# Latent keys ahead of nope queries, output units on five banks with two more weight places, gated rows in two steps, low weights by GpSimd in halves

## The reference

```python
# latent attention (8 heads): q from a 384-wide latent, k and v from a 128-wide one
q = (rms_norm(cq, q_norm_g) @ w_uq).reshape(B_, T, MLA_HEADS, dqk)      # nope 128 + rope 64
kv = (rms_norm(ckv, kv_norm_g) @ w_ukv).reshape(B_, T, MLA_HEADS, 256)  # k nope 128, v 128
p = jax.nn.softmax(q @ k * scale); o = p @ v
y = jnp.concatenate([a, b], axis=-1) * jax.nn.silu(gate)
x = x + y @ w_out

# retention (4 heads of 256 keys, 512 values)
o = ((o - mu) * lax.rsqrt(var + NORM_EPS)).reshape(B_, T, RET_V) * gn_g
x = x + (o * jax.nn.silu(gate)) @ w_out

return rms_norm(x, final_norm_g)
```

## Time and profile before

| | |
|---|---|
| median of 3 runs | 1727.99 us (1726.3 to 1729.07) |
| profiled execution | 1727.9 us, its span 1726.0 us |
| busy: PE, DVE, ACT, POOL | 1655.1, 1036.1, 798.5, 710.0 us |
| DMA | 166.87 MB, mean 97 GB/s |
| matmuls | 7340, granted clock 0.988 of full in the mean |

### The profile page before, as it was taken

One profiled execution on the slowest core, in us unless ns is written; L12 is line 12 of the kernel. 1 busy time (PEld: TensorE's weight loads), 2 busy tenths in 40 slices (PEclk: granted clock), 3 DMA queues, 4 the chain that ended last, 5 costly groups with the idle time before them and its releaser, 6 DMA issues.

```text
span 1726.0 us, 19471 instructions
## 1 busy us (share of the span) xinstructions
PE 1655.1 (96%) x7340; PEld 1343.7 (78%) x7340; DVE 1036.1 (60%) x1173; ACT 798.5 (46%) x1001; POOL 710.0 (41%) x325
## 2 busy tenths in 40 slices
PE   3999999999989999999999999999899999999997
PEld 2778787877778888888887888777788787887875
DVE  6777788777637918816633767566337564255642
ACT  2665565666444425423342333666554443244442
POOL 1233343433355444444464443444364252442523
PEclk7999999999989999999999999999999999999999
DMA  9333333332233332332322231211133131331312
GB/s 363 134 111 123 122 116 117 96 124 86 73 104 98 96 99 86 101 131 90 97 83 90 88 104 60 70 54 55 38 98 98 37 110 40 109 96 42 105 49 73
DMA packets 46460, 166.87 MB, mean 97 GB/s; under 512 B 5152, under 2 KB 5280, under 8 KB 45856
## 3 DMA queue, kind: packets, MB, share of 16 engines
q1 hardware_dynamic: 46368, 165.63, 29.4%
HBM read 163.52 MB, written 2.10 MB: 96 GB/s over the span
## 4 chain that ended last, share of the span: by engine, by line
PE 84%; DVE 11%; ACT 2%; issue 1%; DMA 1%; POOL 1%; SPq 0%; DVEq 0%; ACTq 0%
PE lin L625 15%; PE lin L627 15%; PE lin L626 15%; PE big L625 7%; PE big L627 7%; PE big L626 7%; DVE scr L1538 1%; DVE cq_lo L1640 1%; DVE tmp L1667 1%; DVE tmp L2130 1%; PE big L742 1%; DVE tmp L1686 1%; PE big L744 1%; PE big L1033 1%; PE big L1032 1%
## 5 line engine op out<-in xcount | busy, mean ns | idle before, releaser
L599 POOL TENSOR_TENSOR w_lo<-raw,w_hi 128x1024 fp32r<-128x1024 f32 (+1 forms) x215 | 530.7, 2472 | 730.5 <-ACT w_hi L1069 730.3
L625 PE MATMUL lin<-h_hi,w_hi 128*128 128x512 f32 x952 | 375.5, 394 | 6.9 <-POOL w_lo L599 3.9
L627 PE MATMUL lin<-h_hi,w_lo 128*128 128x512 f32 x952 | 371.5, 390 | 0.0
L626 PE MATMUL lin<-h_lo,w_hi 128*128 128x512 f32 x952 | 371.2, 390 | 0.0
L1069 ACT ACTIVATE w_hi<-raw 128x1024 fp32r<-128x1024 f32 (+1 forms) x215 | 223.9, 1041 | 161.0 <-PE m_b L643 49.2
L625 PEld LDWEIGHTS lin<-h_hi,w_hi 128*128 128x128 f32 x952 | 179.1, 188 | 46.4 <-POOL w_lo L599 6.5
L627 PEld LDWEIGHTS lin<-h_hi,w_lo 128*128 128x128 f32 x952 | 179.0, 188 | 38.0
L626 PEld LDWEIGHTS lin<-h_lo,w_hi 128*128 128x128 f32 x952 | 179.2, 188 | 37.0 <-issue 0.7
L599 POOL TENSOR_TENSOR qk_hl<-raw,qk_hl 128x1024 fp32r<-128x1024 f32 (+1 forms) x44 | 109.4, 2490 | 164.7 <-ACT qk_hl L1069 164.7
L625 PE MATMUL lin<-y_hi,w_hi 128*128 128x512 f32 x324 | 127.3, 393 | 5.6 <-DVE y_lo L2135 3.0
L627 PE MATMUL lin<-y_hi,w_lo 128*128 128x512 f32 x324 | 126.1, 389 | 0.0
(11 more groups left out here) (455 smaller groups left out, 3217.1 us busy)
## 6 DMA issues: line engine op xcount, KB each, us to landing
raw<-weights SPq DMA_DIRECT2D x245, 512.0 KB, 3.6
slab<-ada SPq DMA_DIRECT2D x32, 512.0 KB, 4.5
scr<-ada SPq DMA_DIRECT2D x16, 512.0 KB, 6.3
raw<-weights SPq DMA_DIRECT2D x10, 256.0 KB, 2.8
x<-x_t SPq DMA_DIRECT2D x2, 1024.0 KB, 6.1
out_t<-scr SPq DMA_DIRECT2D x8, 256.0 KB, 2.0
raw<-weights SPq DMA_DIRECT2D x4, 448.0 KB, 3.4
rgw<-rg_w SPq DMA_DIRECT2D x1, 1024.0 KB, 7.3
```

Of the source, the lines that this page charges most:

```text
L599: nc.gpsimd.tensor_tensor(lo[:, 0:w], raw[:, s, 0:w], hi[:, 0:w].bitcast(F32), ALU.subtract).then_inc(w_split, 1)
L625: nc.tensor.matmul(psum_of(n), wh, hi(k), start=(k == 0), stop=False)
L626: nc.tensor.matmul(psum_of(n), wh, lo(k), start=False, stop=False)
L627: last = nc.tensor.matmul(psum_of(n), wl, hi(k), start=False, stop=(k == nk - 1))
```

## The change

1. GpSimd makes the low part of an entry wider than 512 in two instructions. The first raises `w_half`, for which nobody waits; the second raises `w_split`.
2. For the first three groups of residual units the squares are added two entries later in GpSimd's stream.
3. In latent attention `kn` comes ahead of `qn`, on every engine. ScalarE copies weights once in each head, behind both high parts, at most three entries past the gate's, and no more at the head's end.
4. `a_out` units take five banks. Two more weight places, in `cq_hi` and `cq_lo`, are open from `a_out` 0 to `rv` 2, free once `qn` 7 is done. Parts of units 2 and 3 stand before and behind the last value products; PE waits for all eight residuals before retention.
5. In retention ScalarE calls `split_ahead` between the second and the third gated row.
6. The four gated rows use four buffers, and VectorE makes the next product before the low part.
7. The last norm: ScalarE premultiplies rows 3, 4 and 5 by the gain, writes the root to `m_b` (PSUM) and then to `rstd`; VectorE multiplies five rows, GpSimd three.

```diff
 def home_plan():
+    windows = ((("w_out", 3), ("p_out", 6), None), (("a_out", 0), ("rv", 2), ("qn", HEADS - 1)))
...
-WIDE = ("w_out", "ff_g", "ff_v", "ff_down", "kr", "cq", "ckv", "u", "pool", "pgate", "p_out")
+WIDE = ("w_out", "ff_g", "ff_v", "ff_down", "kr", "cq", "ckv", "u", "pool", "pgate", "p_out", "a_out")
...
+        if (kind, j) == ("a_out", 0):
+            turn[ring] = 0
...
 # GpSimd
+                if w > 4 * P:
+                    nc.gpsimd.tensor_tensor(lo[:, 0:4 * P], raw[:, s, 0:4 * P], hi[:, 0:4 * P].bitcast(F32),
+                                            ALU.subtract).then_inc(w_half, 1)
+                at = 4 * P if w > 4 * P else 0
+                nc.gpsimd.tensor_tensor(lo[:, at:w], raw[:, s, at:w], hi[:, at:w].bitcast(F32),
                                         ALU.subtract).then_inc(w_split, 1)
                 for r, f in enumerate(OUT_UNITS):
-                    if PACK[UNIT[f]] + 1 + NR <= e < PACK[UNIT[f]] + 6 + NR:
-                        add_square(r, e - NR - PACK[UNIT[f]])
+                    m = e - PACK[UNIT[f]] - (NR + SPARE if r < 3 else NR)
+                    if 1 <= m < (7 if r < 3 else 6):
+                        add_square(r, m)
...
+            pool.wait_ge(out_gained, len(OUT_POOL))
+            pool.wait_ge(norm_rooted, 8)
+            for k in OUT_POOL:
+                nc.gpsimd.tensor_tensor(scr[:, k], scr[:, k], rstd[:], ALU.mult).then_inc(out_pool, 1)
...
 # PE
+                unit("kn", h, lambda k: cq_hi[:, 3], lambda k: cq_lo[:, 3])
                 unit("qn", h, CH, CL)
-                unit("kn", h, lambda k: cq_hi[:, 3], lambda k: cq_lo[:, 3])
...
             shares_turned(g, 3)
+            pe.wait_ge(p_exp, 4 * HEADS)
+            unit("a_out", 2, YH, YL, part=range(3))
             latent_products(g)
+            unit("a_out", 2, YH, YL, part=range(3, 7))
+            unit("a_out", 3, YH, YL, part=range(7))
             for m in range(8):
                 unit("a_out", m, YH, YL, ready=None if m else mixed_values,
-                     part=range(7, DK) if m < 2 else None)
+                     part=range(7, DK) if m < 4 else None)
+            pe.wait_ge(resa_done, 8)
...
 # ScalarE, latent attention
-                split_ahead(UNIT[("agate", h)])
+                split_ahead(UNIT[("agate", h)], 3)
...
-                split_ahead(following)
+            split_ahead(UNIT[("a_out", 0)])
...
 # ScalarE, gated rows
-                    nc.scalar.activation(y_hi[:, 4 * (h % 2) + c], tmp[:, c % 2], ACT.Copy).then_inc(yr_high, 1)
+                    nc.scalar.activation(y_hi[:, 4 * (h % 2) + c], tmp[:, c], ACT.Copy).then_inc(yr_high, 1)
                     act.wait_ge(yr_high, counted(yr_high))
+                    if c == 1:
+                        split_ahead(UNIT[("r_out", 8 * (h // 2)) if h % 2 else ("rq", 2 * h + 2)])
...
+            nc.scalar.activation(m_b[:], rstd[:], ACT.Exp, scale=-0.5).then_inc(norm_rooted, 1)
+            act.wait_ge(norm_rooted, counted(norm_rooted))
+            nc.scalar.activation(rstd[:], rstd[:], ACT.Exp, scale=-0.5).then_inc(norm_rooted, 1)
...
 # VectorE, last norm
-            for k in range(DK):
-                v.scalar_tensor_tensor(out=scr[:, k], in0=x[:, k], scalar=p_("final_norm_g", k), in1=rstd[:],
+            for k in OUT_DVE:
+                v.scalar_tensor_tensor(out=scr[:, k], in0=x[:, k], scalar=p_("final_norm_g", k), in1=m_b[:],
```

More of the change, by code:

```diff
@@ L102, in ring_plan @@
     for h in range(HEADS):
-        units += [("qn", h, 3), ("kn", h, 1)]
+        units += [("kn", h, 1), ("qn", h, 3)]
         if h % 2 and h < HEADS - 1:
@@ L216, in build @@
         w_high = sem("w_high")
+        w_half = sem("w_half")
         w_split = sem("w_split")
@@ L1057, in _, with split_ahead @@
             issued = [0]
-            def split_ahead(n):
-                while issued[0] < NE and (PRIOR[issued[0]] is None or PRIOR[issued[0]] < n):
+            def split_ahead(n, entries=NE):
+                while issued[0] < min(NE, PACK[n] + entries + 1) and (PRIOR[issued[0]] is None or PRIOR[issued[0]] < n):
                     e = issued[0]
```

92 lines of the change are left out of this document (56 added, 36 removed).

## The result

The changed kernel takes 1708.47 us in the median of 4 runs (1707.64 to 1710.79), the kernel before 1728.42 (1726.30 to 1729.07): a ratio of 0.9889, 95% interval 0.9872 to 0.9906. That is 20 us less; the forecast was 16.3 less, 1711.6. The profiled execution of the changed kernel is the slowest of its four (1710.79); its span is 1709.0 us, 17.0 under that of before.

What follows compares the result with a forecast made beforehand. TensorE bounds the kernel, busy 1655.1 of 1726.0 us, so only its 71 us of standing can be won. The terms sum to -15.2, with tails of -1.1 to -16.3: 1727.9 becomes 1711.6 us, range 1704 to 1720.

Steps and rivals of the forecast that it cites:

- Low weights in halves: GpSimd's split low parts: -4.4 us at first-stage suffix waits, +0.3 at the first norm apply, +0.2 for two later tiles.
- The other three are 1.1 each and vanish, and of the longest 1.1 go: First-stage suffix waits of PE: three end, the longest of 1.9 us loses 1.1; together -4.4 us.
- Elsewhere VectorE often has two such instructions in a row, which then meet one half each, and nothing is won: Outside the first stage, the halved low parts were to win VectorE nothing; the first norm apply was put at +0.3 us.
- (c): Rival: slower, as halves hold VectorE twice; 20 us lost against 16.3 won, 1731 us; chance 0.07.
- (d): Rival: halves do nothing for VectorE, as GpSimd keeps its hold over both; 1716 us; chance 0.08.
- Squares two entries later: At w_out's norm: root 0.3 us earlier, norm apply meets no tile, 0.8; -1.1 us. At ff_down and a_out 0.
- Keys ahead of queries: Latent attention: -2.9 us at the low-part waits, against later shares in heads 2, 4 and 6; net -2.0 us.
- a_out: End of attention: three PE waits of 4.1 us vanish, the residual wait before retention adds 1.1; net -3.0 us.
- Gated rows: Retention: -2.3 us for tile waits at heads 1 and 3, -2.3 for row waits, with 0.55 and 0.2 left.
- Final norm: Final multiplications shared by VectorE and GpSimd: 1.8 us earlier by engines alone, but stores limit the gain to -0.6 us.
- three signs of being wrong: First stage to 430 us not 4 us shorter, new waits for `w_lo`, or VectorE's busy time up by over 10 us.
- Rival (a): The waits move on, at the convolution or next scores and in attention; 4.4 + 2.0 us back, 1718 us; chance 0.15.

Runs made afterwards that it cites:

- e1: The changed kernel with GpSimd making each low part in one whole instruction again; 1719.12 us, ratio 0.9936 to the kernel before.
- e2: The kernel before with only the low parts made in halves; 1722.66 us against 1730.21, ratio 0.9959.
- e5: The changed kernel with the latent values' high parts ahead of two weight copies in attention head 0, and the residual wait later in retention head 0; 1706.39 us, ratio 0.9882.
- e10: The changed kernel with queries ahead of keys again on every engine, weight copies still behind both high parts; 1709.22 us, ratio 0.9896 to the kernel before.
- e6: The changed kernel with each gated row's low part right behind its product again, in one step; 1711.99 us, ratio 0.9913 to the kernel before.
- e7: The changed kernel without the weight copies between the second and third gated row; 1707.23 us, ratio 0.9884 to the kernel before.
- e9: The changed kernel with gated rows in one step and no weight copies between them; 1716.24 us, ratio 0.9934 to the kernel before.
- e4: The changed kernel with TensorE running the second modulation's 16 small matmuls ahead of the second norm's sum; 1707.52 us, ratio 0.9875 to the kernel before.

## Why the prediction was right, step by step

The sign, the place of nearly every gain and the total were right (16.3 forecast, 20 measured). Its terms were worse than its sum: three were too small, three too large, one was right. In the table of stretches some 6 us more than forecast (tails counted) stand against 5 us less, so that the profiled spans differ by 17.0 us where 16.3 were forecast is in part luck.

1. **Low weights in halves**, forecast -4.4, +0.3 and +0.2. Measured -7 to -8 in e1 and e2. "VectorE will get in after the first half, 1.1 us earlier" held, for another instruction than the one I named. "The other three are 1.1 each and vanish, and of the longest 1.1 go" came out (three are gone, the longest fell from 1.94 to 0.71), but by another path: I reckoned the stop inside `cq_lo` alone, and not that the stop before it in the same chain moves `cq_lo` out of the tile's way. With their tails these four are 5.0 us. The step that failed is "Elsewhere VectorE often has two such instructions in a row, which then meet one half each, and nothing is won": in e2 the waits for shares in heads 2 and 4 are gone (1.5 us) and the four retention heads' scores gain 0.8. The "0.2 us later per tile" was too small where GpSimd works back to back with VectorE (0.56 in e2), but in the changed kernel the two tiles concerned are no longer waited for. GpSimd's 72 us more (e2 against before) are otherwise hidden. Rivals (c) and (d) are out by VectorE's 53 us less.
2. **Squares two entries later**, forecast -1.1 at w_out. Measured -1.0 where the clock held and +0.6 to +0.7 where it fell. My times for the sum and the root hold to 0.1 us in e5; missing was what 2.4 us of standing can do to the clock. "For ff_down and a_out a whole unit (5.4 us) lies between the last product and the sum: 0" failed at a_out. There the last square stands behind GpSimd's tile for a later entry and came 1.3 us late:

```profile
1278.00 1.26 POOL L595 TENSOR_TENSOR sq_sum<-sq_sum,sq_act 128x512 f32<-128x512 f32 x1
1279.32 1.12 PE L700 MATMUL m_a<-sq_sum,cst 128*128 128x512 f32 x2 [1.30 <-POOL sq_sum L595]
```

The change's own new places let those tiles start earlier and stand in the way.

3. **Keys ahead of queries**, forecast -2.0. Measured -1.65. The odd heads gave 0.65 each, and the waits for shares in heads 2 and 4 rose by 0.13 (to 0.87 and 0.86), not by 0.35. In head 0 the 0.96 was won and 1.1 lost at once: I had counted the copy ahead of the turned queries, but not that in head 0 the same two copies stand ahead of the values' high parts. e10 shows that the copy's place alone gives 0.24 of the 0.65, and the order the rest on top of it.
4. **a_out**, forecast -4.1 + 1.1. The waits vanished (with tails 4.9 us) and the residual's came at 0.85 us, 1.0 from start to start. The -2.2 of the stretch is short of -3.0 only through the late square (1.5 from start to start). No run undid this edit, so the five banks, the two places and the parts of units 2 and 3 are not told apart.
5. and 6. **Gated rows**, forecast -2.3 - 2.3, with 0.55 and 0.2 left. Measured from start to start -2.9 for the tiles and -3.8 for the rows, nothing left, and 0.8 in the scores' product that I hadn't seen as a wait (0.08 and 0.11 us at two matmuls, four times). The step that failed is "edit 5 puts a weight copy (1.06) in ScalarE's queue and a tile under the last two low rows, which have two SBUF inputs: 1.4 us lost"; e6 shows no loss. And the sum hid an interaction: I gave the tiles' gain to the copies, but the two steps bring it too (e7, e9).
7. **Final norm**, forecast -0.6. Measured -0.6, at a DMA share of 1.0.

Of what was to be seen, two things did not come: `cq_lo` at 2.6 us (it is 2.46 in the first head and 1.49 in the others), and waits for shares above 1 us (they are 0.87). Of the three signs of being wrong none came: to 430 us the kernel is 4.15 us shorter, there is no new wait for `w_lo`, and VectorE is busy less. Rival (a), that the waits move on, did happen at three places: the sum of squares, the values, the second sum. They are 4.8 us in the list of waits, of which 2.4 came back at the norm's `h_lo` (2.5). In the kernel before that wait was:

```profile
PE big L702 <- DVE h_lo L1565: 4.9, 1, 4.9
```

## What to carry to other kernels

Where two engines block each other instruction by instruction, cut the longer instructions, and look for the gain in the whole chain, not in the instruction that shows the longest block: once the chain is out of phase with the other engine's instruction, the block falls on another, shorter one. Count what the extra instructions cost where the cut engine is itself waited for. Follow every copy or square that is moved past others to each consumer behind it, in the first and the last pass of a loop above all, where the neighbours differ. Two edits that remove one wait are to be undone together as well as apart before either is given the gain.

## What the runs showed of the hardware

- A short stand of PE can be followed by a stretch at 1.2 GHz, and whether it is, differs between executions of the same code. Behind the same wait (2.2 to 2.4 us) the clock held in six profiles and fell in two. It costs 1.3 to 2.9 us each time, at the first products 1.4 to 2.9. A wait removed can therefore be worth nearly twice its length (2.4 us of standing and 1.7 us of slow sums in the changed kernel).
- In e4 the clock fell behind 16 one-column matmuls (1.6 us, by the profile all busy) and 0.7 us of standing: 1.00, then 0.82, then 0.50. It is one profile, so it shows no rule.
- GpSimd and VectorE alternate by instruction also when both have the next one ready. Cut in two, a tile costs GpSimd 2.9 us in place of 2.5, and VectorE's 1280-wide `cq_lo` went from 3.41 to 1.61 us in the mean, while the 512-wide one behind it went from 0.69 to 1.59.
- Stores to HBM from one core ran at 373 to 387 GB/s for four microseconds once two engines prepared the rows; with VectorE alone they ran at 320 to 354.
